# Rotated units of an attention encoder: the swap of halves moves into the middle of the unit after next

## The reference

```python
h = _rmsnorm(x, g_in)
proj = h @ w_in
(a_q, a_k, a_v, a_z, b_q, b_k, b_v, b_qi, b_ki, b_wi, b_z,
 c_q, c_z, gates) = jnp.split(proj, _split_points(), axis=-1)
a_q = _rope(a_q.reshape(b, s, SWA_HEADS, HEAD_DIM), cos, sin)
...
y_a = _sliding_window_sink_attention(a_q, a_k, a_v, attn_sinks)
...
y_b = _dsa_sparse_attention(b_q, b_k, b_v, b_qi, b_ki, b_wi)
...
y_c = _memory_cross_attention(...)
ys = jnp.stack([y_a * jax.nn.silu(a_z), y_b * jax.nn.silu(b_z), y_c * jax.nn.silu(c_z)], axis=2)
u = jnp.einsum('bsnc,ncd->bsnd', ys, w_branch)
merged = jnp.sum(jax.nn.sigmoid(gates.reshape(b, s, N_BRANCH, D_MODEL)) * u, axis=2)
return x + merged @ w_out
```

```python
def _rope(x, cos, sin):
    x1, x2 = jnp.split(x, 2, axis=-1)
    return jnp.concatenate([x1 * cos - x2 * sin, x2 * cos + x1 * sin], axis=-1)
```

## Time and profile before

| | |
|---|---|
| median of 3 runs | 2774.99 us (2771.25 to 2780.04) |
| the profiled execution: its time | 2774.9 us |
| its span, from the first to the last instruction | 2773.1 us |
| TensorE busy | 2507.8 us (90%) |
| VectorE busy | 1789.3 us (65%) |
| ScalarE busy | 1379.0 us (50%) |
| GpSimd busy | 411.9 us (15%) |
| swaps of halves on TensorE (two products each) | 52, 22.4 + 21.0 us busy |

### The profile page before, as it was taken

How to read it: one execution, slowest core, us unless ns; L and a number is a source line. 1 busy time by engine, 2 the same in 40 slices (tenths; PEclk the granted TensorE clock), 3 DMA queues, 4 the chain that set the end, 5 groups by cost and what they waited for, 6 DMA issues and landing times.

```text
span 2773.1 us, 36879 instructions
## 1 busy us (share of the span) xinstructions
PE 2507.8 (90%) x12861; PEld 2076.2 (75%) x12861; DVE 1789.3 (65%) x3613; ACT 1379.0 (50%) x2785; POOL 411.9 (15%) x397
## 2 busy tenths in 40 slices
PE   6998999998999999998889999999988879888897
PEld 5776888776778888887677778888666667777776
DVE  6567676234767777226878788732678888776652
ACT  5555645343646444225756545532566674545541
POOL 5434353440000000100000000010000000000010
PEclk8999999999999999999999999999999999999999
DMA  5656584785353522564343421156423324111125
GB/s 189 216 181 205 175 283 148 251 276 178 125 166 122 173 79 69 193 224 160 99 160 110 149 92 47 46 178 224 169 82 123 113 99 160 61 54 50 58 87 187
DMA packets 172583, 399.32 MB, mean 144 GB/s; under 512 B 13808, under 2 KB 96752, under 8 KB 162416
## 3 DMA queue, kind: packets, MB, share of 16 engines
q1 hardware_dynamic: 172400, 396.96, 43.4%
HBM read 308.31 MB, written 88.60 MB: 143 GB/s over the span
## 4 chain that ended last, share of the span: by engine, by line
PE 49%; DVE 22%; ACT 16%; issue 10%; DMA 1%; POOL 1%; DVEq 0%; SPq 0%; ACTq 0%; POOLq 0%
PE bank L892 36%; PE TR L788 5%; ACT signs L1057 5%; PE PV L859 4%; ACT prob L1022 3%; ACT prob L1032 3%; DVE ptL L1443 2%; DVE prob L1402 2%; ACT ptH L1046 2%; DVE nmx L1412 2%; DVE score L1668 2%; PE bank L799 1%; PE bank L800 1%; DVE zs L1478 1%; DVE above L1529 1%
## 5 line engine op out<-in xcount | busy, mean ns | idle before, releaser
L892 PE MATMUL bank<-hH,pairs 128*128 128x512 f32 (+1 forms) x3584 | 1160.3, 394 | 17.8 <-DVE zs L1510 7.6
L892 PEld LDWEIGHTS bank<-hH,pairs 128*128 128x128 f32 x3584 | 679.6, 192 | 156.9 <-issue 18.7
L892 PE MATMUL bank<-hL,pairs 128*128 128x512 f32 (+2 forms) x1792 | 704.6, 393 | 0.0
L1057 ACT ACTIVATE signs<-score,bits 128x384 int8<-128x384 f32 (+7 forms) x256 | 335.8, 1312 | 214.3 <-DVE bits L1548 201.3
L1443 DVE TENSOR_TENSOR ptL<-TR,ptH 128x512 fp32r<-128x512 f32 (+1 forms) x384 | 257.0, 671 | 267.9 <-ACT ptH L1046 264.6
L892 PEld LDWEIGHTS bank<-hL,pairs 128*128 128x128 f32 (+1 forms) x1792 | 344.0, 192 | 64.9
L1046 ACT ACTIVATE ptH<-TR 128x512 fp32r<-128x512 f32 (+1 forms) x384 | 219.8, 577 | 328.8 <-PE TR L788 327.8
L1529 DVE TENSOR_SCALAR_CACHE_REDUCE above<-score,bits 128x256 uint8<-128x256 f32 (+10 forms) x280 | 348.2, 1243 | 9.5
L788 PE MATMUL TR<-identR,prob 128*128 128x128 f32 x1480 | 233.5, 279 | 91.2 <-ACT prob L1032 50.2
L788 PEld LDWEIGHTS TR<-identR,prob 128*128 128x128 f32 x1480 | 180.0, 142 | 166.6 <-ACT prob L1032 63.9
L892 PE MATMUL bank<-ysH,pairs 128*128 128x512 f32 x768 | 258.2, 398 | 10.2 <-issue 5.4
(11 more groups left out here) (213 smaller groups left out, 3645.6 us busy)
## 6 DMA issues: line engine op xcount, KB each, us to landing
pairs<-w_split SPq DMA_DIRECT2D x444, 512.0 KB, 3.5
w_split<-pairs SPq DMA_DIRECT2D x74, 1024.0 KB, 5.0
raw<-in_w_in SPq DMA_DIRECT2D x106, 256.0 KB, 5.6
xs<-in_x SPq DMA_DIRECT2D x4, 2048.0 KB, 9.1
rows<-in_x SPq DMA_DIRECT2D x16, 512.0 KB, 4.9
table<-trig SPq DMA_DIRECT2D x48, 128.0 KB, 2.9
raw<-in_w_branch SPq DMA_DIRECT2D x24, 256.0 KB, 5.6
out<-rows SPq DMA_DIRECT2D x3, 2048.0 KB, 7.5
```

The source lines that it names most:

```text
L892: done = nc.tensor.matmul(PJ[st.u + half * up][0:min(st.width, P), 0:st.n_tok], lhs, rhs[:, row, 0:st.n_tok], start=(n % 12 == 0 and (up o ...
L1057: nc.scalar.activation(signs[:, 0:keys], score[:, tt, 0:keys], ACT.Sign, bias=thr.bitcast(F32)[:, tt:tt + 1], scale=-1.0, accum_out=cnt[:, ...
```

## The change

In a section with z units beside it (index, A, B) the list is written in another order. Each unit is issued in two steps: `first_half` (12 products, TensorE alone knows this step) and the unit itself (the other 12, and the work of all other engines). Between the two stands the swap of the unit two before, where until now the swap of the unit one before stood behind the whole unit. So the swap of the last rotated unit moves from behind the first z unit into the middle of the second, and its halve behind the second. The section of the memory values keeps its order. The squares of the rows (`row_squares`) now stand ahead of the halve of qi 1.

```diff
@@ -71,6 +71,7 @@
+        self.begun = False
@@ -148,16 +149,24 @@
     def turned(specs, beside=(), counting=None, selecting=None, tables=False, finishing=None):
 
-        units = []
-        for n_unit in range(len(specs) + 1):
+
+        units, behind = [], 2 if beside else 1
+        for n_unit in range(len(specs) + behind):
+            now = None
             if n_unit < len(specs):
                 role, src, col, more = specs[n_unit]
-                units.append(unit(role, src, col, **more))
+                units.append(unit(role, src, col, into=[], **more))
+                now = units[-1]
             elif beside:
-                role, src, col, more = beside[0]
-                unit(role, src, col, **more)
-            if n_unit:
-                st = units[n_unit - 1]
+                role, src, col, more = beside[n_unit - len(specs)]
+                now = unit(role, src, col, into=[], **more)
+            if now and behind == 2:
+                steps.append(Step("first_half", unit=now))
+                now.begun = True
+            elif now:
+                steps.append(now)
+            st = units[n_unit - behind] if n_unit >= behind else None
+            if st:
                 if st.role in ("av", "mv", "kv", "kiw"):
                     steps.append(Step("turn", unit=st, tr=take("tr")))
                     f_freed.append(("tr_full", n["tr"]))
@@ -167,6 +176,9 @@
                     if st.role in ("kv", "kiw"):
                         f_freed.pop()
                     f_freed.append(("tr_full", swaps[-1] + 1))
+            if now and behind == 2:
+                steps.append(now)
+            if 0 < n_unit <= len(specs):
                 if counting is not None and n_unit < len(specs):
                     select_bits(counting, PER_TURN)
                 if selecting is not None:
@@ -174,14 +186,12 @@
                         steps.append(Step("select", g=selecting, i=phase))
                 if finishing is not None:
                     finish(finishing, 2 * n_unit - 2, 2 * n_unit)
+                    if n_unit == len(specs):
+                        steps.append(Step("row_squares", g=finishing, tr=n["tr"], tt=0, tiles=NT))
                 if tables:
                     steps.append(Step("tables", i=3 + n_unit))
-                if st.role in ROPED:
-                    steps.append(Step("halve", unit=st, k=st.k, tr=swaps[-1]))
-        if finishing is not None:
-            steps.append(Step("row_squares", g=finishing, tr=n["tr"], tt=0, tiles=NT))
-        for role, src, col, more in beside[1:]:
-            unit(role, src, col, **more)
+            if st and st.role in ROPED:
+                steps.append(Step("halve", unit=st, k=st.k, tr=swaps[-1]))
         if finishing is not None:
             steps.append(Step("row_scale", g=finishing, tr=n["tr"]))
 
@@ -907,8 +917,10 @@
+                elif st.kind == "first_half":
+                    projected(st.unit, 0, PRODUCTS // 2)
                 elif st.kind == "unit":
-                    projected(st, 0, PRODUCTS)
+                    projected(st, PRODUCTS // 2 if st.begun else 0, PRODUCTS)
```

## The result

The changed kernel takes 2816.55 us in the median of five runs (2811.99 to 2822.29), the kernel before 2773.51 (2770.51 to 2780.04): ratio 1.0152, 95% interval 1.0138 to 1.0166, so 43 us or 1.5% slower. The forecast was 2810 us with a range of 2793 to 2825. The profiled execution of the changed kernel took 2822.29 us and that of before 2774.9; this pair is 47.4 us apart, 2.3 of which lie ahead of the first rotated unit (the wait for the memory rows at the start was 15.0 us instead of 12.7), where the two kernels do the same.

What follows compares the result with a forecast made beforehand. The prediction took TensorE's own work (2507.8 us) plus some 265 us of waits as the bound. Terms of 13.5 + 6.7 + 7 + 2.7 + 5.5 = 35.4 us on 2774.9 gave 2810 us, range 2793 to 2825.

Steps and rivals of the forecast that it cites:

- late halves at the sections' ends: Section ends: the last swap's halve comes one unit later, so the indexer's and attention's scores wait for it.
- the B sections: B sections: last halve ahead of the first masked maximum, 2.2 us in group 1, little in the others; sum +2.7.
- The index sections: Indexer's first unit starts later: net +4.5 us in each of groups 1 to 3 (+13.5), +6.7 in group 0.
- The A sections: One more halve (2.75 us) ahead of the last rotated sum, less 1.0 won at the start: +1.8 each, +7.
- half restarts: A sections: half a clock restart counted for each, 3 us in all, because ScalarE's exponentials are the later end there.
- The clock: TensorE runs at half rate after longer joined waits: restarts in index group 0, B of group 1 and A, +5.5 us.
- ScalarE's stop: Each unit: copy fH waits mid-unit about 3.3 us for the previous swap; cost from nothing to 3.3 us each time.
- What would show it: Signs: swap waits under 8 us, section-end waits grow, fH waits for the swap, VectorE's A cycle stays 8.25 us.
- (a): Rival: section-end halves are hidden and the 48.9 us of waits are really won, 2726 us; chance 0.05.
- (b): Rival: waits only change place, gains matched by equal losses at section ends, 2783 us at most; chance 0.07.
- (d): Rival: group 0's weight conversions stand behind ScalarE's wait and make weights late, +20 us, 2830 us; chance 0.13.

Runs made afterwards that it cites:

- single-part run: New order in the four index sections alone, A and B sections as in the kernel before: 2796.80 us, +21.4 on before, ratio 1.0078.
- experiment 7: Changed kernel plus 16 unread products on TensorE at each of nine section-end waits: 2812.46 us, +38.8 on the kernel before, ratio 1.0140.
- experiment 4: Changed kernel with two buffers for fH and fL, so ScalarE's copy waits for an older swap: 2800.88 us, +27.2 on the kernel before.
- B-only kernel: New order in the four B sections alone, index and A sections as in the kernel before: 2785.35 us, +9.9 on before, ratio 1.0038.
- experiment 5: Changed kernel, but each section's last swap stays behind the first z unit and the row squares keep their old place: 2783.45 us, +9.8 on before.

## Why the prediction was right, and where it was not

The direction, the size and the main reason (late halves at the sections' ends) held: 2816.55 us measured, 2810 forecast, inside the range.

The terms summed to 35.4 us, 7.6 less than measured, and 6.2 of these are the B sections.

*The index sections.* Right to fractions of a us in group 1, from which the terms were taken. There TensorE reached the counting point 12.0 us later than before (672.95 against 660.99) where the group had begun 16.5 us later (first output products, 590.10 against 573.59): 4.5 won, for which 4.6 was worked out; the squares began 12.2 us after it (12.1), the indexer's unit 24.5 (24.6). In groups 2 and 3 the distance had been 13.8 and not 15.5 us before, and grew to 24.5 and 24.2, by 10.6 and 10.4 instead of 9.1. The single-part run gave 21.4 us (18.0 to 25.5) where the terms had 13.5 + 6.7 + 1.5 = 21.7; that they meet so closely is partly luck. That the wait for the stored rows swallows the half clock there fits experiment 7 in group 1, and within 1 us in group 3; group 2 cannot tell.

*The A sections.* 8.6 us for 10. VectorE's count in group 1 came every 5.4 us in the first turn, which has no halve yet, and then every 8.45 us (forecast 8.25); the scores waited 5.74 us (near 6). That ScalarE's stop costs nothing there agrees with the text ("The move leaves that cycle as it is") and not with what I expected of experiment 4, 4.9 us ahead of the last halves. The reason given for half restarts was wrong: behind the waits it is not "ScalarE's exponentials" that are busy (1.25 of 4 us) but VectorE (3.20).

*The B sections* are the term of the sum that was mis-sized: "Sum +2.7" and 1 for a restart, measured 9.9. I had counted in A that one more halve stands ahead of the last rotated sum, and in B looked only at the first masked maximum; "in groups 2 and 3 VectorE's selection passes set the end of the section" left out that the halve is queued behind these passes, ahead of the sum. In the B-only kernel the B sections of the four groups ended 3.8, 2.1, 2.2 and 1.4 us later than before, 9.5 in all: the 2.2 us that I had worked out for group 1 alone came about in every group, more or less. "The unit behind hides it" (said of group 0) failed: in the changed kernel TensorE waited there 2.4 us where it had not waited. The halve in the queue is one part of the reason: with the last swap alone moved, the B sections cost 2.3 us, as the 2.7 said, and with two buffers 5.6; the rest of the 13.3 in the changed kernel goes with ScalarE's stop.

*The clock.* 5.5 us forecast, about 4 measured with an interval that reaches from nothing to 10, and some 4 more if the harm in group 2 is added: not contradicted, not sharp. The half clock lasts longer than I took (4 us and more behind nine waits), and costs less for each; that this is because it lies beside a busy VectorE is read from the windows, not tested.

*ScalarE's stop.* Given as 0 to 3.3 us a time and about 10 us of the total in the index sections; 16 us measured in all, a good part of it in the B sections, where I had said that everything behind it has slack. ScalarE stood idle 5.6 us ahead of each fH copy that waited (105.8 / 19), not 3.3.

*What would show it.* fH waits for the swap's second product: yes, 105.8 us. The growth at section ends: near 6 in A of group 1, yes (5.74); at the indexer's first unit it was less than said: the waits were 6.0, 4.2, 4.1 and 5.1 us in groups 0 to 3, after 1.1, 1.5, 0 and 0, for growths of "about 8" and "over 5". VectorE's cycle: 8.45 and not 8.25. The swap's waits "under 8 us": wrong, 17.7. All nine that remained lie in A sections, where VectorE is late, and the text itself had said that the move leaves that cycle as it is; the bound contradicted it.

*The rivals.* (a), waits really won, is refuted by sign; experiment 5 shows that they are won in front of the moved swaps (14.8 us) and lost again at the next one. (b) needed the indexer's unit 4.6 us later after the counting point; it was 9.0. (d) is not what happened to the sum, but its place stays open: by the first scores of attention C, less the difference at the start, group 0's index section cost 10.5 us in the changed kernel's execution and 5.1 in the index-only kernel's, for a term of 6.7 + 1.5.

## What to carry to other kernels

A wait in front of an instruction is worth moving it only if the time that it gives is not taken from its consumer's side: follow the chain behind the moved step to the end of the section, where no next unit covers it any more. Count every copy that is queued ahead of the last link on each engine, and count it in every section of the same shape, also where another wait seems to set the end. A delay at one of these links can cost little alone and much together with another. And look at who shares the resource that a step frees: the swap gained 14 to 21 us by moving a few products earlier, into more waiting of its own, for the most part because the transposes behind the unit then found their bank free.

## What was not expected of the hardware

Nine waits of 4 to 6 us were each followed by 4 us or more at a granted clock near 0.50 (1.2 GHz), as in the windows above, while in the kernel before, with waits of at most 1.4 us ahead of attention A's scores, the same windows have 1.00. The length of the wait does not settle it: in the kernel with only the last swap moved, the indexer's unit waited 2.17 us in each of groups 1, 2 and 3, and the four us behind had a granted clock of 0.57, 1.00 and 1.00. Sixteen products whose result nobody reads, issued inside the wait, kept the clock at 1.00 behind it in three of four A sections, with 1.2 us of the wait left in group 3, and in all four index sections. Giving TensorE its full clock back at seven of these nine places changed the time by about 4 us, or some 8 with the 4 that the extra products cost in group 2: half of its rate over at least 36 us (9 x 4) cost little; in the A sections VectorE was 80% busy beside it (3.20 of 4 us).
